# x transposed as it lands, its RMS scale applied to the first projections' outputs, and the first two weight slabs loaded in pieces

## The reference, cut to what matters

```
def rms_norm(x, g):
    y = x32 * lax.rsqrt(jnp.mean(x32 * x32, axis=-1, keepdims=True) + EPS)
    return y * g
h = rms_norm(x, mix_norm_g[0])
gb, gc, hc, q, k, v, g = split_cols(h @ w_in, EVEN_SPLITS)    # 512 columns each
a = gb * conv(gc * hc)          # three taps along the tokens
q, k = rotary(q), rotary(k)     # then retention over q, k, v; silu(g) gates its output
```

## Time and profile before

| | us |
|---|---|
| median of 3 runs | 1642.45 (1641.81 to 1644.15) |
| the profiled execution, its own time | 1642.63 |
| its span | 1640.7 |
| TensorE busy | 1614.0 (98%) |
| VectorE busy | 1271.0 (77%) |
| ScalarE busy | 1036.0 (63%) |
| POOL busy | 55.5 (3%) |

### The profile page before, as it was taken

The page is one execution under the profiler, slowest core; times in us unless marked ns, Lnnn a source line. Parts: engine busy times, 40 slices in busy tenths (PEclk is TensorE's granted clock), DMA queues, the critical chain, the costliest instruction groups (busy, mean ns, idle before and its releaser), DMA issues.

```text
span 1640.7 us, 22659 instructions
## 1 busy us (share of the span) xinstructions
PE 1614.0 (98%) x8508; PEld 1378.6 (84%) x8508; DVE 1271.0 (77%) x1070; ACT 1036.0 (63%) x908; POOL 55.5 (3%) x52
## 2 busy tenths in 40 slices
PE   7999999999999999999999999999999999999997
PEld 6998989998887798888788888888888888888885
DVE  7776646454567675799888888888888888889897
ACT  5443445544356544677777777777777777777775
POOL 1000000000000101100000000000000000000010
PEclk9999999999999999999999999999999999999999
DMA  9644535555554354899999999999979999999994
GB/s 355 206 155 154 160 123 180 180 182 199 161 192 140 129 217 174 286 377 356 371 389 371 384 384 372 377 390 370 383 289 357 383 390 368 392 371 369 382 395 162
DMA packets 226030, 474.71 MB, mean 289 GB/s; under 512 B 7698, under 2 KB 52964, under 8 KB 225972
## 3 DMA queue, kind: packets, MB, share of 16 engines
q1 hardware_dynamic: 221552, 459.01, 77.7%
q0 software_dynamic: 3104, 10.66, 1.9%
q10 hardware_dynamic: 1316, 4.24, 0.6%
HBM read 466.01 MB, written 7.87 MB: 289 GB/s over the span
## 4 chain that ended last, share of the span: by engine, by line
PE 88%; issue 5%; DVE 3%; ACT 2%; DMA 1%; POOL 1%; ACTq 0%; POOLq 0%; SPq 0%; DVEq 0%
PE ps L2313 34%; PE ps L2336 16%; PE ps L1845 15%; PE ps L1811 9%; PE ps L1831 4%; PE ps L2074 4%; PE ps L2321 1%; DVE w_lo L393 1%; ACT w_hi L389 1%; PE ps L1986 1%; PE ps L2006 1%; DMA ta<-xn,rden 1%; DMA raw<-in_ev_w_in 0%; PE ps L2100 0%; PE ps L1940 0%
## 5 line engine op out<-in xcount | busy, mean ns | idle before, releaser
L393 DVE TENSOR_TENSOR w_lo<-raw,w_hi 128x2048 fp32r<-128x2048 f32 x430 | 980.0, 2291 | 223.7 <-ACT w_hi L389 222.5
L389 ACT ACTIVATE w_hi<-raw 128x2048 fp32r<-128x2048 f32 x430 | 823.6, 1918 | 296.7 <-PE ps L2313 110.9
L2313 PE MATMUL ps<-w_hi,e_hi 128*128 128x512 f32 x896 | 355.6, 397 | 1.0 <-DVE w_lo L393 0.8
L2313 PE MATMUL ps<-w_hi,e_lo 128*128 128x512 f32 x896 | 349.8, 390 | 0.0
L2313 PE MATMUL ps<-w_lo,e_hi 128*128 128x512 f32 x896 | 349.3, 390 | 0.0
L2313 PEld LDWEIGHTS ps<-w_hi,e_hi 128*128 128x128 f32 x896 | 168.4, 188 | 38.5 <-DVE w_lo L393 3.2
L2313 PEld LDWEIGHTS ps<-w_hi,e_lo 128*128 128x128 f32 x896 | 168.2, 188 | 36.0
L2313 PEld LDWEIGHTS ps<-w_lo,e_hi 128*128 128x128 f32 x896 | 168.5, 188 | 33.1
L2336 PE MATMUL ps<-w_hi,at_hi 128*128 128x512 f32 x448 | 175.9, 393 | 0.4 <-DVE w_lo L393 0.4
L2336 PE MATMUL ps<-w_hi,at_lo 128*128 128x512 f32 x448 | 174.6, 390 | 0.0
L2336 PE MATMUL ps<-w_lo,at_hi 128*128 128x512 f32 x448 | 174.5, 390 | 0.0
(11 more groups left out here) (359 smaller groups left out, 1717.1 us busy)
## 6 DMA issues: line engine op xcount, KB each, us to landing
raw<-in_moe_w_up SPq DMA_DIRECT2D x112, 1024.0 KB, 7.9
raw<-in_moe_w_gate SPq DMA_DIRECT2D x110, 1024.0 KB, 7.5
raw<-in_moe_w_down SPq DMA_DIRECT2D x110, 1024.0 KB, 7.2
raw<-in_xa_wkv SPq DMA_DIRECT2D x16, 1024.0 KB, 5.2
raw<-in_ev_w_in SPq DMA_DIRECT2D x14, 1024.0 KB, 9.5
raw<-in_od_w_in SPq DMA_DIRECT2D x12, 1024.0 KB, 5.1
raw<-in_ffd_w_gate SPq DMA_DIRECT2D x11, 1024.0 KB, 5.4
raw<-in_ffd_w_up SPq DMA_DIRECT2D x11, 1024.0 KB, 5.3
```

Source lines behind the costliest of these rows:

```text
L389: nc.scalar.activation(w_hi[:, n % CUT, :], at_, ACT.Copy).then_inc(hi_cut, 1)
L393: nc.vector.tensor_tensor(w_lo[:, n % CUT, :], place(n, r, behind)[0], w_hi[:, n % CUT, :].bitcast(F32), ALU.subtract).then_inc(lo_cut, 1)
L2313: mm = T.matmul(ps[:, bank, :], s, m, start=(h == 0 and k == 0 and j == 0), stop=(h == 1 and k == 3 and j == 2))
```

## The change

SyncE loads the constants first, then x in two column halves and slabs 0 and 1 in two pieces each; the ten small gain transfers move from ScalarE's queue to SyncE's, between the two slabs of evk, and mem moves behind evk. ScalarE's queue carries the positions (one to a partition, in two transfers) and one gain vector, rows0. TensorE transposes rows0, the constant 8 times, and the unscaled x half by half (`turn_raw`); the second half stands between the second and third k row of slab 0. The squares, the root and r (`rkeep`) come later. r is multiplied into cos and sin (for q and k), into the copies of evv and evg, and, as a row over tokens (`r_row`, made by a matmul of ones with a diagonal), squared into `ev_c` and once into `ev_u` on POOL. The angles and sines move ahead of the first slab's cuts. Allocations and unchanged lines are left out (four places shortened):

```diff
 def _(sp):
-    sp.dma_start(X[:, :, :], x[0].rearrange("(t p) n -> p t n", p=P)).then_inc(in_x, 16)
+    def x_half(h, arrived):
+        c = slice(512 * h, 512 * h + 512)
+        sp.dma_start(X[:, :, c], x[0].rearrange("(t p) n -> p t n", p=P)[:, :, c]).then_inc(arrived, 16)
     sp.dma_start(const[:, :], consts[:, 0:3 * P + 56]).then_inc(in_const, 16)
+    x_half(0, in_x)
+    for i in range(2):
+        s = slabs["evq"][i]
+        for half_, arrived in ((0, first_in[i]), (1, raw_in[i])):
+            sp.dma_start(shaped(raw[:, i, 1024 * half_:1024 * half_ + 1024], 2),
+                         s[:, 2 * half_:2 * half_ + 2, :]).then_inc(arrived, 16)
+        if i == 0:
+            x_half(1, in_x2)
     for name, k in STREAM:
-        if name in ("fgu", "fdn"):
+        if name in ("evq", "fgu", "fdn"):
...
             load(sp, n + i, s)
-        if name == "evq":
-            sp.wait_ge(in_row, 160)
+            if name == "evk" and i == 0:
+                for row, v in (("mem", mem_norm_g), ("x0", mix_norm_g[0]), ("x1", mix_norm_g[1]),
+                               ("xa0", xa_norm_g[0]), ("xa1", xa_norm_g[1]), ("ffn", ffn_norm_g[0]),
+                               ("moe", ffn_norm_g[1]), ("ret", ev_ret_gn_g[0]), ("dif", od_gn_g[0])):
+                    r, k = ROWS[row], v.shape[0] // P
+                    sp.dma_start(rows[r:r + k, :], v.rearrange("(k p) -> k p", p=P)).then_inc(in_row, 16)
+                sp.dma_start(rows[ROWS["conv"]:N_ROWS, :],
+                             ev_conv_w[0].rearrange("j (k p) -> (j k) p", p=P)).then_inc(in_row, 16)
+        if name == "evk":
...
                                             ALU.mult).then_inc(xg_mul, 1)
+        if name == "mem":
+            pool.wait_ge(setup_s, 3)
+            nc.gpsimd.tensor_tensor(r_row2, r_row, r_row, ALU.mult).then_inc(rb_rdy, 1)
+        if name == "ret":
+            pool.wait_ge(acc_free, BANKS["evc"] + 6)
+            nc.gpsimd.tensor_tensor(ev_u, ev_u, r_row.unsqueeze(1).broadcast_to([P, 4, 256]),
+                                    ALU.mult).then_inc(conv_r, 1)
...
         act.wait_ge(act_link, links[0])
-    act.dma_start(pos_i[:, :], positions[0].rearrange("(k p) -> k p", p=P)).then_inc(in_pos, 16)
-    for name, v in (("mem", mem_norm_g), ("x0", mix_norm_g[0]), ("x1", mix_norm_g[1]), ("xa0", xa_norm_g[0]),
-                    ("xa1", xa_norm_g[1]), ("ffn", ffn_norm_g[0]), ("moe", ffn_norm_g[1]),
-                    ("ret", ev_ret_gn_g[0]), ("dif", od_gn_g[0])):
-        r, k = ROWS[name], v.shape[0] // P
-        act.dma_start(rows[r:r + k, :], v.rearrange("(k p) -> k p", p=P)).then_inc(in_row, 16)
-    act.dma_start(rows[ROWS["conv"]:N_ROWS, :],
-                  ev_conv_w[0].rearrange("j (k p) -> (j k) p", p=P)).then_inc(in_row, 16)
+    for t in range(2):
+        act.dma_start(pos_i[:, t:t + 1],
+                      positions[0, t * P:(t + 1) * P].rearrange("(p o) -> p o", o=1)).then_inc(in_pos, 16)
+    act.dma_start(rows0[:, :], mix_norm_g[0].rearrange("(k p) -> k p", p=P)).then_inc(in_row0, 16)
...
                 events[i]()
+    def first_cut(i, c0, c1, done):
+        nc.scalar.activation(w_hi[:, i, c0:c1], raw[:, i, c0:c1], ACT.Copy).then_inc(done, 1)
     act.wait_ge(pool_link, 1)
-    nc.scalar.activation(mx[:, 15:16], half[:, 0:1], ACT.Square).then_inc(act_link, 1)
-    act.wait_ge(in_x, 16)
-    nc.scalar.activation(rot[:, :, :].rearrange("p a n -> p (a n)"), X[:, 0, :], ACT.Square,
-                         accum_out=sums[:, 0:1]).then_inc(n_sq, 1)
+    nc.scalar.activation(mx[:, 15:16], half[:, 0:1], ACT.Sin).then_inc(act_link, 1)
+    act.wait_ge(setup_v, 1)
+    turn_hi("x0", a_hi, tiles=range(2))
+    act.wait_ge(first_in[0], 16)
+    first_cut(0, 0, 512, first_hi)
+    turn_hi("x0", a_hi, tiles=range(2, 4))
+    first_cut(0, 512, 1024, first_hi)
     act.wait_ge(raw_in[0], 16)
-    nc.scalar.activation(w_hi[:, 0, 0:1024], raw[:, 0, 0:1024], ACT.Copy).then_inc(first_hi, 1)
-    nc.scalar.activation(w_hi[:, 0, 1024:2048], raw[:, 0, 1024:2048], ACT.Copy).then_inc(hi_cut, 1)
-    act.wait_ge(setup_v, 3)
-    turn_hi("x0", a_hi, tiles=range(4))
-    cut_hi(act, 1)
-    turn_hi("x0", a_hi, tiles=range(4, 8))
-    act.wait_ge(setup_v, 4)
+    first_cut(0, 1024, 2048, hi_cut)
+    act.wait_ge(setup_v, 2)
...
     nc.scalar.activation(cos[:, :, :], ang[:, :, :], ACT.Sin, scale=0.5).then_inc(setup_s, 1)
-    stage("evq", 2)
+    act.wait_ge(first_in[1], 16)
+    first_cut(1, 0, 1024, first_hi)
+    turn_hi("x0", a_hi, tiles=range(4, 8))
+    act.wait_ge(raw_in[1], 16)
+    first_cut(1, 1024, 2048, hi_cut)
+    cut_hi(act, 2)
+    act.wait_ge(in_x, 16)
+    act.wait_ge(in_x2, 16)
+    squares("x0", X)
+    cut_hi(act, 3)
     stage("evk", 2)
+    act.wait_ge(setup_t, 3)
+    nc.scalar.activation(r_row, ps[:, 4, 0:256], ACT.Copy).then_inc(setup_s, 1)
...
     nc.scalar.activation(ev_g, ev_g, ACT.Silu).then_inc(g_silu, 1)
-    act.wait_ge(acc_free, BANKS["evc"] + 6)
+    act.wait_ge(conv_r, 1)
...
         ins.then_inc(acc_free, w)
-    dve.wait_ge(in_pos, 16)
-    V.tensor_copy(pos_f[:, :], pos_i[:, :]).then_inc(setup_v, 1)
-    dve.wait_ge(setup_t, 1)
-    V.tensor_copy(pos[:, :], ps[:, 7, 0:2]).then_inc(setup_v, 1)
-    dve.wait_ge(in_x, 16)
-    V.tensor_tensor_reduce(u[:, 9216:10240], X[:, 1, :], X[:, 1, :], 1.0, 0.0, ALU.mult, ALU.add,
-                           sums[:, 1:2]).then_inc(n_sq, 1)
-    norm("x0", X, tat)
-    dve.wait_ge(setup_t, 2)
-    V.tensor_copy(cols[:, :], ps[:, 6, 0:N_ROWS]).then_inc(setup_v, 1)
-    dve.wait_ge(first_hi, 1)
-    V.tensor_tensor(w_lo[:, 0, 0:1024], raw[:, 0, 0:1024], w_hi[:, 0, 0:1024].bitcast(F32),
-                    ALU.subtract).then_inc(first_lo, 1)
-    dve.wait_ge(hi_cut, 1)
-    V.tensor_tensor(w_lo[:, 0, 1024:2048], raw[:, 0, 1024:2048], w_hi[:, 0, 1024:2048].bitcast(F32),
-                    ALU.subtract).then_inc(lo_cut, 1)
-    dve.wait_ge(setup_v, 3)
-    turn_lo("x0", a_hi, a_lo, tiles=range(4))
-    cut_lo(dve, 1)
-    turn_lo("x0", a_hi, a_lo, tiles=range(4, 8))
-    dr = ROWS["dif"]
-    link(V.tensor_scalar(cols[:, dr:dr + 8], cols[:, dr:dr + 8], 1.0 - LAM0, None, ALU.mult))
-    for t in range(2):
-        link(V.tensor_scalar(ang[:, t, :], freq, pos[:, t:t + 1], None, ALU.mult))
...
     big = 12582912.0
+    dve.wait_ge(in_pos, 32)
+    link(V.tensor_copy(pos[:, :], pos_i[:, :]))
+    dve.wait_ge(in_const, 16)
+    for t in range(2):
+        link(V.tensor_scalar(ang[:, t, :], freq, pos[:, t:t + 1], None, ALU.mult))
     link(V.tensor_scalar(turnsb[:, :, :], ang[:, :, :], 1.0 / (2 * math.pi), None, ALU.mult))
+    dve.wait_ge(setup_t, 1)
+    r0 = ROWS["x0"]
+    V.tensor_copy(cols[:, r0:r0 + KT], ps[:, 2, 0:KT]).then_inc(setup_v, 1)
...
     V.tensor_scalar(ang[:, :, :], ang[:, :, :], 3.141592, -3.141592, ALU.min, ALU.max).then_inc(setup_v, 1)
+    def first_rest(i, c0, c1, whole, count, done):
+        dve.wait_ge(whole, count)
+        V.tensor_tensor(w_lo[:, i, c0:c1], raw[:, i, c0:c1], w_hi[:, i, c0:c1].bitcast(F32),
+                        ALU.subtract).then_inc(done, 1)
+    turn_lo("x0", a_hi, a_lo, tiles=range(2))
+    first_rest(0, 0, 512, first_hi, 1, first_lo)
+    turn_lo("x0", a_hi, a_lo, tiles=range(2, 4))
+    first_rest(0, 512, 1024, first_hi, 2, first_lo)
+    first_rest(0, 1024, 2048, hi_cut, 1, lo_cut)
...
     link(V.tensor_scalar(cos[:, :, :], cos[:, :, :], -2.0, 1.0, ALU.mult, ALU.add))
+    first_rest(1, 0, 1024, first_hi, 3, first_lo)
+    turn_lo("x0", a_hi, a_lo, tiles=range(4, 8))
+    first_rest(1, 1024, 2048, hi_cut, 2, lo_cut)
+    cut_lo(dve, 2)
+    dve.wait_ge(setup_t, 2)
+    V.tensor_copy(cols[:, 0:r0], ps[:, 7, 0:r0]).then_inc(dve_link, 1)
+    links[0] += 1
+    link(V.tensor_copy(cols[:, r0 + KT:], ps[:, 7, r0 + KT:N_ROWS]))
+    dr = ROWS["dif"]
+    link(V.tensor_scalar(cols[:, dr:dr + 8], cols[:, dr:dr + 8], 1.0 - LAM0, None, ALU.mult))
+    dve.wait_ge(n_sq, 2)
+    means("x0", 2, D)
+    V.tensor_copy(rkeep[:, :], rstd[:, 0:2]).then_inc(n_out, 2)
+    dve.wait_ge(n_out, 2)
+    for t in range(2):
+        for v in (cos, sin):
+            link(V.tensor_scalar(v[:, t, 0:32], v[:, t, 0:32], rkeep[:, t:t + 1], None, ALU.mult))
+    for t in range(2):
+        V.tensor_scalar(r_diag[:, t * P:(t + 1) * P], ident, rkeep[:, t:t + 1], None,
+                        ALU.mult).then_inc(setup_v, 1)
...
         ins.then_inc(acc_free, 2)
-    stage("evq", 2)
+    cut_lo(dve, 3)
...
     rotate(acc("evk", 0, 2), ev_kr, RH, 32, 0, rotated)
-    stage("evv", 2, {1: lambda: freed(V.tensor_copy(ev_v, acc("evv", 0, 2)), 2)})
+    def scaled(dst, name):
+        for t in range(2):
+            ins = V.tensor_scalar(dst[:, t, :], acc(name, 0, 2)[:, t, :], rkeep[:, t:t + 1], None, ALU.mult)
+        freed(ins, 2)
+    stage("evv", 2, {1: lambda: scaled(ev_v, "evv")})
     turn_lo("mem", m_hi, m_lo)
-    dve.wait_ge(setup_s, 3)
+    dve.wait_ge(setup_s, 4)
...
```

(42 more changed lines are left out.)

12 lines of the change are left out of this document (9 added, 3 removed).

## The result

The changed kernel takes 1667.04 us (median of 4 runs, 1665.54 to 1669.58), the kernel before beside it 1642.44 (1641.81 to 1644.15). The ratio is 1.0147, with a 95% interval of 1.0135 to 1.016. The forecast was 1639.7 with a range of 1638.0 to 1643.0, so it missed by 27 us, and on a side to which it gave 3 in 100. The profiled execution was the slowest of the four (1669.58).

The account below looks back on a forecast made before the run. TensorE, busy 98% of the span, was taken as the bound, so time is evk's start at 25.96 us plus its work. Opening 3.8 less 0.43 and 0.65 gave 2.7 us less: 1639.7 us, range 1638.0 to 1643.0.

Parts of the forecast that it names:

- Sum: 3.8 - 0.43 - 0.65 = 2.7 us less: Whole kernel: opening's gain of 3.8 us less the fp32 matmul's 0.43 and the POOL product's 0.65.
- R: Opening: moment when rows0 has landed and TensorE can start; taken as 4.8 us, range 3.7 to 6.4.
- the aside on the queues: Opening: DMA engines take queues a packet at a time, so rows0 lands at about 4.6, forecast 0.2 us lower.
- The clock's rival: First matmuls: clock still low, 4 us at half pace lose 2.0, whole time 1641.7 us; chance 0.28.
- R + 17.4: End of the opening: evk's start on TensorE, 17.4 us after rows0 lands, at 22.2 us.
- Nothing else ends later: Opening: ScalarE and VectorE keep up; VectorE ends slab 3's w_lo at R + 20.9, needed at R + 22.9.
- signs of being wrong: Evk before 21 or after 24 us, or a wait on w_lo, setup_s or the banks between evk and evc.
- (a): After the opening: the fp32 matmul that spreads the scale adds 0.43 us to TensorE's stream.
- (d): Ahead of the retention scores: POOL's 128x1024 product takes 2.5 us, costing 0.65 after a slack of 2.0.
- (b): After slab 3: ScalarE waits for the fp32 matmul before squaring mem; hidden with 1.2 us to spare.
- (c): Scalings of evv and evg: two VectorE instructions instead of one, about 0.1 us each, hidden; evc's copy costs nothing.

Follow-up runs that it names:

- c_low_first: Changed kernel at the old places, slab 3's high part cut ahead of ScalarE's squares, its low part ahead of VectorE's columns' copy; 1645.6 us, once.
- d_no_product: Changed kernel at the old places without GpSimd's product of the convolution's output with the row scale; 1641.61 us, once.
- a_after_old_addr: Changed kernel with 448 bytes of padding, so the region and m_hi start where they did before; 1643.74 us, ratio 1.0004 to the kernel before.
- d_open: Changed kernel at the old places: rows0 first, more dummy transposes, positions' chain behind slab 0's low parts, slab 3 cut earlier; 1640.53 us, ratio 0.9990 to before.

## Why the prediction was wrong

- **The sum left out a term.** "Sum: 3.8 - 0.43 - 0.65 = 2.7 us less" counts instructions that are added, removed and moved, each by a duration of before. It takes for granted that the 8000 others keep theirs. They didn't: the diff's four lines on pos_i, pos_f, rows0 and rkeep moved an operand of some 4600 matmuls of 512 columns by 448 bytes, and that alone made the kernel before 22.8 us slower. No rival had it. It is 23.3 of the 27.3 us of the miss; the other 4.0 (1643.74 against 1639.7) lie in the next three points. The lines stood in the diff; an allocation that changes size should have been a step of the working.
- **R was too early.** "I take R = 4.8"; rows0 landed at 5.90, within the stated 3.7 to 6.4 (5.9 to 6.7 in the 13 traces with this opening); the 4.6 of the aside on the queues was further off, and the long wait for the small rows, said there to agree with it, spoke for a late R. x's first half landed at 6.7 and not at 5.0, which cost nothing as TensorE had its transposes of the constant to do until 8.0. Every start of the opening followed; the first matmul came at R + 5.6 (forecast 5.25).
- **The clock's rival came true in nine of 13 traces** (0.28, "4 us at half pace lose 2.0"): in the profiled execution the first twelve matmuls took 4.35 us where they take 3.04 at the full clock, so 1.3 us were lost; over the traces it is 0 to 2.4. It is most of evk at R + 19.15 instead of R + 17.4.
- **"Nothing else ends later" failed.** VectorE was to end slab 3's low part at R + 20.9, that is 26.8; it ended at 30.7. The working placed the row statistics there and not the wait ahead of them, for a transpose that TensorE does behind slab 1. c_low_first shows it: 0.8 us on the chain. These are two of the prediction's own signs of being wrong: evk after 24 (25.05), and a wait on w_lo between evk and evc (0.5 us in two). Later landing 1.1, first matmul 0.4, clock 1.3 and late cut 0.8 make 3.6 of the 4.0 us.
- **(a) and (d) were right**: 0.43 for the fp32 matmul; the product took 2.41 us (forecast 2.5) and the wait ahead of the scores was 0.6 (0.65), 0.5 by d_no_product. (By the Trainium skill, GPSIMD Engine Reference, section Performance versus the Vector engine, the estimate was 2.3.) **(b) and (c)** were hidden as said; no wait stands there.
- Without the place the change comes out level (a_after_old_addr, 1.0004 of before, some 1643.1 us, or 1643.74 as measured), just above the range. That this lies near the forecast is no support for its 2.7 us, since "no change" at 1642.4 lies in the range too. The change gives 1.9 us once the order of its opening is mended (d_open, 1640.53 against 1642.45).

## What to carry to other kernels

A change that adds, drops or resizes an SBUF tile moves everything allocated behind it; before costing it, print the addresses of the matmuls' two operands before and after, and hold them with padding while the rest is measured. When a time changes by more than all waits together, compare the start-to-start step of the matmuls that the diff doesn't touch, since their mean length hides it. And an engine's program order carries waits along: what is placed behind a wait for another engine's late instruction is late too.

## What the hardware showed that I hadn't expected

- The step between fp32r matmuls depends on the distance of the two operands in SBUF modulo 256 bytes: 227 to 234 ns for the experts' 128x512, 113 to 120 for a_hi's 128x256, at the full clock and with no wait. For these kernels that is the difference between 1632.7 and 1670.2 us with the same instructions.
- The two kinds want different distances (0 and 192), and at 192 the second kind has two steps, 113.3 and 117.8 ns, one of which holds for 100 us and more; executions differ in which.
- A small transfer's landing depends on its place in its queue: behind the positions rows0 landed at 5.9 to 6.7 us; asked for first, it landed at 2.6 (four traces), and the positions behind it at 8.1 to 8.3 instead of 5.9 to 6.8.
